# Hybrid decoder layer on one core: a sixth expert buffer elsewhere in SBUF, a new order in the last expert units, and two tiles of the last stage on VectorE alone

## The chip, the cores and the metric

The kernel runs on one core of a Trainium2 chip. The metric is the device time of one execution in microseconds. Engines: TensorE (PE in the profile; its weight loads are PEld), VectorE (DVE), ScalarE (ACT), GpSimd (POOL), SyncE (SP). SBUF and PSUM are the on-chip memories; a "bank" is one of eight PSUM banks of 128 x 512 f32.

## What is computed

One decoder layer over 1024 tokens of width 1024, all f32. Four mixers share the layer's input, then comes attention to a fixed memory, then a mixture of experts, then a final norm. The change touches the last two:

```python
h = _rmsnorm(x, norm_ffn[l])
x = x + hier_moe(h, w_rg[l], b_rg[l], w_re[l], b_re[l], w_e_gu[l], w_e_dn[l])
...
return _rmsnorm(x, norm_final)
```

`hier_moe` has each token choose one of 4 groups of 8 experts and two experts in it, each with a weight. An expert multiplies the row by `w_gu` (1024 x 512), takes `silu(gate) * up` (256 values), and multiplies by `w_dn` (256 x 1024). The two results, weighted, are added to x.

## The kernel before

**Up to the experts.** The first 750 us or so are the mixers, then come attention to the memory and the routing. The residual rows x2 (8 tiles of 128 tokens x 1024, 4 MB) are summed in the arena, one large SBUF tensor, at `o_bc`. For every tile SyncE stores the normed rows to DRAM (`xn_d`) and then x2 itself (`x2_d`, shown as `x_d` in the profile; `sp_tail`, L1197 and L1199), since the sixth weight buffer (`GU_AT[5]`, `DN_AT[5]`) lies over x2.

**The expert stage.** Tokens are sorted into 84 blocks of 32 slots. Four blocks make a unit, 21 units (`UN`) in all, numbered 0 to 20. Experts are ordered by load; the first have 3 or 4 blocks, the last 13 have 2 each. So the last units take two experts each: unit 18 the experts at places 26 and 27, unit 19 those at 28 and 29, unit 20 those at 30 and 31 (here simply "expert 28" and so on). Expert e uses buffer e mod 6. For one unit:

- GpSimd gathers 128 token rows from `xn_d` (L1836), TensorE transposes them (`tr`, L1569), VectorE scales them (`tokens`, L1347).
- `gate_up`: products with the gate-up weights into bank 2 or 6 (L1583), 2 MB of weights per expert.
- ScalarE takes silu (L1242), VectorE multiplies (L1356), TensorE transposes the result (`act_tr`, L1592), ScalarE copies it (L1246).
- `down`: products with the down weights, 1 MB per expert, into banks 4 and 5 (L1606).
- ScalarE and VectorE copy the result out (L1251, L1363), GpSimd scatters the rows to `y_d` in DRAM (L1847).

TensorE's order is written out in `pe_experts`: gate_up(u), act_tr(u-1), tr(u+1), down(u-1). ScalarE's and VectorE's orders (`act_experts`, `dve_experts`) have silu and gating of u ahead of the copies of u-1. SyncE loads weights (`sp_experts`, L1122 for gate-up, L1127 for down): when gate_up(u) is done, the gate-up weights for the buffers that become free; then, when down(u-1) is done, the down weights. At the end this gives the order of issue: gate-up 28 and 29, down 26 and 27, gate-up 30 and 31, down 28 and 29, down 30 and 31. All go through one hardware queue.

When down(18) is done SyncE issues `x2_back` (L1229), which brings x2 back into other places (`xb`). Then it reads a flag of slot overflow (not set here), loads the gain of the final norm (`fin_g`, L1989) and waits for all scatters (`pass_end`, L1150 and L1151).

**The last stage**, per tile m of 8: SyncE loads the two expert rows of each token (`yg[m]`, 1 MB, L1994; four at once, then one for each that lands). TensorE puts x2 into two banks by a product with the identity (`start`, L1960; the first four tiles before any y is there) and adds the first expert row times its weight by a product with a diagonal (`w_diag`, L1971). VectorE adds the second (L1941, two halves), ScalarE squares and takes the root (L1984, L1985), VectorE inverts (L2374) and scales by root and gain (L1952), SyncE stores (L1998, the last tile in halves, L2002). VectorE's order is: sum of m, then scaling of m-1.

## Time and profile before

| | |
|---|---|
| median of 3 runs | 1184.95 us (1183.56 to 1187.94) |
| the profiled execution's own time | 1186.36 us |
| its span in the trace | 1184.6 us |
| TensorE busy | 1116.2 us (94%) |
| VectorE busy | 538.4 us (45%) |
| ScalarE busy | 351.5 us (30%) |
| GpSimd busy | 117.3 us (10%) |
| DMA | 204.74 MB, mean 173 GB/s |
| share of the final chain | TensorE 73%, VectorE 10%, DMA 5% |

A busy share is a mean over stages that have different limits. The chain of waits, followed back from the last instruction, says which work ended last at each point; the windows give busy time, granted clock and DMA share of a stretch; the timeline gives single instructions, and in brackets how long the engine was idle before one and what ended that.

### The profile page before, as it was taken

How to read it: one execution, taken by the hardware profiler on the slowest of the kernel's cores; microseconds unless marked ns; L12 is line 12 of the kernel's file. 1: busy time of each engine (PE TensorE's matmuls, PEld its weight loads, DVE VectorE, ACT ScalarE, POOL GpSimd, SP SyncE). 2: the span in 40 equal slices, each digit the busy share in tenths (PEclk: the TensorE clock that was granted, in tenths of full speed). 3: DMA queues.
4: the chain of work that ended last, by engine and by line, in shares of the span. 5: the costliest groups of instructions: out<-in, count | busy, mean ns of one | idle time of the engine just before them, and what ended most of it. 6: DMA issues, size and time to landing. Idle time of an engine off the chain costs nothing.

```text
span 1184.6 us, 16485 instructions
## 1 busy us (share of the span) xinstructions
PE 1116.2 (94%) x6487; PEld 615.4 (52%) x6487; DVE 538.4 (45%) x1199; ACT 351.5 (30%) x676; POOL 117.3 (10%) x148
## 2 busy tenths in 40 slices
PE   6999999999999899988799999999999999999777
PEld 6545744444744589875465444456653333333223
DVE  6876333324399635596672222235442212121117
ACT  4114631111676423203664100165301111111004
POOL 2000012221000000001010000022111111111000
PEclk9999999999999899999989999999999999999889
DMA  8111022131113443330034000446388999999988
GB/s 285 37 57 56 14 82 69 64 97 50 36 36 134 190 129 84 132 144 1 3 141 178 0 1 1 148 173 236 117 290 342 413 390 421 421 424 421 423 322 353
DMA packets 67894, 204.74 MB, mean 173 GB/s; under 512 B 24573, under 2 KB 41185, under 8 KB 57313
## 3 DMA queue, kind: packets, MB, share of 16 engines
q1 hardware_dynamic: 61104, 186.64, 41.4%
q0 software_dynamic: 6656, 16.95, 3.8%
q8 instruction: 54, 0.88, 0.3%
q14 instruction: 32, 0.25, 0.1%
q10 hardware_dynamic: 48, 0.01, 0.0%
HBM read 171.58 MB, written 37.24 MB: 176 GB/s over the span
## 4 chain that ended last, share of the span: by engine, by line
PE 73%; DVE 10%; DMA 5%; issue 3%; ACT 3%; POOL 0%; SPq 0%; DVEq 0%; POOLq 0%; ACTq 0%
PE bank L2674 20%; PE bank L1583 11%; PE bank L1639 8%; PE bank L1606 5%; PE bank L1701 2%; PE bank L1654 2%; DMA arena<-in_w_e_gu 2%; DMA arena<-x_d 2%; PE bank L2801 2%; PE bank L805 1%; PE bank L916 1%; PE bank L1960 1%; PE bank L1569 1%; PE bank L866 1%; PE bank L853 1%
## 5 line engine op out<-in xcount | busy, mean ns | idle before, releaser
L2674 PE MATMUL bank<-arena 128*128 128x512 f32 (+3 forms) x1032 | 358.0, 506 | 8.1 <-ACT arena L2178 6.8
L2674 PEld LDWEIGHTS bank<-arena 128*128 128x128 f32 x1032 | 196.9, 192 | 163.0 <-issue 140.7
L1583 PE MATMUL bank<-arena 128*32 128x512 f32 x1344 | 150.4, 599 | 8.3 <-issue 7.3
L1583 PEld LDWEIGHTS bank<-arena 128*32 128x32 f32 x1344 | 44.8, 111 | 109.4 <-issue 109.4
L1639 PE MATMUL bank<-arena 128*128 128x512 f32 x220 | 95.6, 592 | 0.0
L2178 ACT ACTIVATE arena<-bank 128x512 f32<-128x512 f32 (+1 forms) x57 | 28.4, 504 | 167.3 <-PE bank L2674 166.8
L1606 PE MATMUL bank<-arena 128*32 128x512 f32 x672 | 76.5, 595 | 1.4 <-ACT arena L1246 1.4
L1356 DVE TENSOR_TENSOR arena<-arena,bank 128x256 f32<-128x256 f32 x21 | 8.9, 422 | 149.4 <-ACT arena L1242 149.4
L1399 DVE TENSOR_TENSOR arena<-arena,bank 128x512 f32<-128x512 f32 x32 | 22.0, 688 | 100.2 <-PE bank L1639 79.5
L1639 PEld LDWEIGHTS bank<-arena 128*128 128x128 f32 x220 | 41.3, 190 | 49.7 <-issue 49.7
L1242 ACT ACTIVATE arena<-bank 128x256 f32<-128x256 f32 x21 | 8.1, 383 | 156.7 <-PE bank L1583 156.7
L2164 ACT ACTIVATE arena<-arena 128x1024 f32<-128x1024 f32 x18 | 19.0, 1054 | 100.3 <-DVE arena L1399 95.0
L2445 DVE TENSOR_TENSOR arena<-arena,bank 128x512 f32<-128x512 f32 x35 | 23.3, 684 | 50.6 <-PE bank L2674 50.6
L1363 DVE COPY arena<-bank 128x512 f32<-128x512 f32 x21 | 14.5, 691 | 60.3 <-PE bank L1606 60.3
L1606 PEld LDWEIGHTS bank<-arena 128*32 128x32 f32 x672 | 20.0, 109 | 41.5 <-issue 39.2
L1251 ACT ACTIVATE arena<-bank 128x512 f32<-128x512 f32 x21 | 12.5, 597 | 85.8 <-PE bank L1606 85.8
L2615 DVE TENSOR_TENSOR arena<-arena,bank 128x512 f32<-128x512 f32 x24 | 16.5, 685 | 47.4 <-PE bank L2801 47.4
L805 PE MATMUL bank<-arena 64*128 64x128 f32 x448 | 32.7, 300 | 4.2 <-DVE arena L716 2.6
L716 DVE COPY_PREDICATED arena<-levT,bank 128x512 f32<-128x512 int32 x56 | 35.3, 710 | 0.7 <-PE bank L805 0.4
L1836 POOL DMA_INDIRECT arena<-xn_d,arena x21 | 21.4, 1017 | 138.1 <-PE bank L1569 121.5
L805 PEld LDWEIGHTS bank<-arena 64*128 64x128 f32 x448 | 29.6, 207 | 7.2 <-DVE arena L716 4.0
L1701 PE MATMUL bank<-arena 128*128 128x512 f32 x64 | 32.1, 625 | 0.9 <-DVE arena L1399 0.9
(408 smaller groups left out, 1564.2 us busy)
## 6 DMA issues: line engine op xcount, KB each, us to landing
arena<-in_w_e_gu SPq DMA_DIRECT2D x27, 2048.0 KB, 13.2
arena<-in_w_e_dn SPq DMA_DIRECT2D x32, 1024.0 KB, 13.5
arena<-in_w_in SPq DMA_DIRECT2D x11, 1024.0 KB, 5.2
arena<-y_d SPq DMA_DIRECT2D x8, 1024.0 KB, 11.1
arena<-hz_d SPq DMA_DIRECT2D x4, 1792.0 KB, 8.0
pk_d<-arena SPq DMA_DIRECT2D x8, 640.0 KB, 2.9
hz_d<-arena SPq DMA_DIRECT2D x4, 1280.0 KB, 4.9
arena<-in_w_e_gu SPq DMA_DIRECT2D x5, 1024.0 KB
```

What stands on the lines that cost most here:

```text
L716: v.copy_predicated(h_pm[it % 2][:, par], bc(levT[:, lv].bitcast(i32), 1, [P, 4, P]), scores).then_inc(s["h_pm"], 1)
L805: ins = mm(to, hz(it, lv)[rows(par), part], hz(it, lv)[rows(par), part], start=True, stop=True)
L1399: return v.tensor_tensor(part, part, bank[:, :], ALU.add)
L1583: ins = mm(bank[part, :], hgT[:, k, part], w_gu(buf(es[i]), k), start=(k == 0), stop=(k == KT - 1))
L1606: ins = mm(psum[4 + hf][part, :], actT[:, k, part], w_dn[buf(es[i])][:, k, cols], start=(k == 0), stop=(k == FE // P - 1))
L1639: ins = mm(psum[2 + u % 3][:, :], y_of(k, slice(m * P, (m + 1) * P)), wo[:, k, hf * HALF:(hf + 1) * HALF], start=(u >= 3 and k == W_ORDER[0]),
L1654: ins = mm(psum[Q_BANK[u]][:, :], mq[:, k, c * P:(c + 1) * P], hT[:, k, hf * HALF:(hf + 1) * HALF], start=(k == 0), stop=(k == KT - 1))
L1701: ins = mm(psum[3][:, :], m_oT[m % 2][:, c], mo[:, c, hf * HALF:(hf + 1) * HALF], start=(c == 0), stop=(c == CT - 1))
L2178: ins = nc.scalar.activation(dst, psum[PROJ_BANKS[u % 3]][0:rows, cols], ACT.Copy, scale=QK_SCALE if CHUNKS[UNITS[u][0]][1] == col["bq"] a ...
L2445: ins = v.tensor_tensor(to, to, bank, ALU.add)
L2674: ins = mm(psum[PROJ_BANKS[u % 3]][0:rows, 0:n], lhs(k), rhs(k), start=(k == 0), stop=(k == kt - 1))
L2801: ins = mm(psum[7][:, hp(h)], Qp[:, h], y[:, h], start=True, stop=True)
```

## The change

- Tables that are used only up to the routing (`triu`, `triu_s`, `tril_s`, `head_ones`, `levT`, `lru_w`, `memk`, `memv`) become slices of one tensor `early` of 3072 columns. The arena grows by 2048 columns; the space for that comes from halving the space for GpSimd's DMA descriptors (8192 bytes). The sixth buffer lies in `early`, in 1024 columns at the old end of the arena and in the new columns, so it no longer covers x2. `b_rank` and `toks_of` are placed in those 1024 columns.
- x2 is neither stored nor brought back. `y_out`, `yg`, `fin_g` and `w_diag` get other places; `fin_g` is loaded after gate_up(20).
- Before it loads buffer 5 the first time, SyncE waits for `t_r_dve` 6 instead of 4.
- At unit 20 TensorE does act_tr(19) and down(19) first and gate_up(20) then; ScalarE and VectorE likewise copy out unit 19 before silu and gating of unit 20.
- In the last stage tiles 4 and 7 (`SOLO`, the fifth and the last) are summed by VectorE alone, with two operations on 1024 columns in SBUF. TensorE works on the other six.

TensorE at the end of the expert stage, before (bank4, bank5: down; bank2: gate_up(20); bank3: act_tr; e_dn4 and x_cb are the semaphores of the down weights of experts 28 and 29, w_ld0 and w_ld1 those of the gate-up weights of experts 30 and 31):

```order
L1583 MATMUL bank2<-arena 32x512 [waits e_ac,e_ht,w_ld1,w_ld0]
L1583 MATMUL bank2<-arena 32x512 x15
L1583 MATMUL bank2<-arena 32x512 [waits e_ht]
L1583 MATMUL bank2<-arena 32x512 x15
L1592 MATMUL bank3<-ident,arena 128x128 [waits e_ats,e_ac]
L1592 MATMUL bank3<-ident,arena 128x128
L1606 MATMUL bank4<-arena 32x512 [waits e_ats,e_y,x_cb,e_dn4]
L1606 MATMUL bank4<-arena 32x512 x7
L1606 MATMUL bank5<-arena 32x512 x8
L1592 MATMUL bank3<-ident,arena 128x128 [waits e_ats,e_ac]
L1592 MATMUL bank3<-ident,arena 128x128
L1606 MATMUL bank4<-arena 32x512 [waits e_ats,e_y,e_dn1,e_dn0]
```

and with the change:

```order
L1584 MATMUL bank3<-ident,arena 128x128 [waits e_ats,e_ac]
L1584 MATMUL bank3<-ident,arena 128x128
L1598 MATMUL bank4<-arena 32x512 [waits e_ats,e_y,x_cb,e_dn4]
L1598 MATMUL bank4<-arena 32x512 x7
L1598 MATMUL bank5<-arena 32x512 x8
L1575 MATMUL bank2<-arena 32x512 [waits e_ac,e_ht,w_ld1,w_ld0]
L1575 MATMUL bank2<-arena 32x512 x15
L1575 MATMUL bank2<-arena 32x512 [waits e_ht]
L1575 MATMUL bank2<-arena 32x512 x15
L1584 MATMUL bank3<-ident,arena 128x128 [waits e_ats,e_ac]
L1584 MATMUL bank3<-ident,arena 128x128
L1598 MATMUL bank4<-arena 32x512 [waits e_ats,e_y,e_dn1,e_dn0]
```

The block of 32 products into bank2 moves behind the one that waits for e_dn4 and x_cb, and nothing stands any more between it and the last act_tr.

VectorE in the last stage at tile 4, before:

```order
L1941 SCALAR_TENSOR_TENSOR arena<-arena,bank7 128x512 [waits f_p]
L2374 RECIPROCAL rms<-rms 128x1 [waits rms_r]
L1952 SCALAR_TENSOR_TENSOR arena<-arena,rms,levT 128x1024 [waits v_chain]
L1941 SCALAR_TENSOR_TENSOR arena<-arena,bank0 128x512 [waits f_p,x_in0]
L1941 SCALAR_TENSOR_TENSOR arena<-arena,bank1 128x512 [waits f_p]
L2374 RECIPROCAL rms<-rms 128x1 [waits rms_r]
L1952 SCALAR_TENSOR_TENSOR arena<-arena,rms,levT 128x1024 [waits v_chain]
```

and with the change:

```order
L1943 SCALAR_TENSOR_TENSOR arena<-arena,bank7 128x512 [waits f_p]
L2376 RECIPROCAL rms<-rms 128x1 [waits rms_r]
L1954 SCALAR_TENSOR_TENSOR arena<-arena,rms 128x1024 [waits v_chain]
L1935 SCALAR_TENSOR_TENSOR arena<-arena 128x1024 [waits x_in0]
L1937 SCALAR_TENSOR_TENSOR arena<-arena 128x1024 [waits v_chain]
L2376 RECIPROCAL rms<-rms 128x1 [waits rms_r]
L1954 SCALAR_TENSOR_TENSOR arena<-arena,rms 128x1024 [waits v_chain]
```

The two halves that took TensorE's sums from bank 0 and bank 1 become two operations on whole rows in SBUF, the second linked to the first. The same happens at tile 7; all else keeps its order.

```diff
@@ -42,11 +42,10 @@
 
         ident = sb("ident", [P])
         ones = sb("ones", [P])
-        triu = sb("triu", [P])
-        triu_s = sb("triu_s", [P])
-        tril_s = sb("tril_s", [P])
-        head_ones = sb("head_ones", [P])
-        levT = sb("levT", [NL + 1, P])
+        early = sb("early", [3072])
+        triu, triu_s, tril_s, head_ones = [early[:, i * P:(i + 1) * P] for i in range(4)]
+        levT = early[:, 512:1536].rearrange("p (a b) -> p a b", a=NL + 1)
+        lru_w = early[:, 1536:2048].rearrange("p (a b) -> p a b", a=2 * CT)
         negmask = sb("negmask", [P])
         prow = sb("prow", [P])
...
@@ -1032,15 +1031,16 @@
         buf = lambda e: e % NB
         GU = KT * 2 * FE
         GU_AT = [((o_g2, 0, KT),), ((0, 0, KT),), ((EW, 0, KT),), ((o_g1, 0, KT),),
-                 ((o_g3, 0, 4), (o_tmp + 6 * D, 4, 6), (o_cx, 6, 8)), ((o_bc, 0, KT),)]
-        DN_AT = [o_g2 + GU, GU, EW + GU, o_g1 + GU, o_g1 + EW, o_bc + GU]
+                 ((o_g3, 0, 4), (o_tmp + 6 * D, 4, 6), (o_cx, 6, 8)), ((None, 0, 6), (48024 - 1024, 6, 8))]
+        DN_AT = [o_g2 + GU, GU, EW + GU, o_g1 + GU, o_g1 + EW, 48024]
+        piece = lambda off, n: early[:, 0:n] if off is None else arena[:, off:off + n]
         w_dn = [view(o, FE // P, D) for o in DN_AT]
 
         def w_gu(j, k):
 
             for off, k0, k1 in GU_AT[j]:
                 if k0 <= k < k1:
-                    return arena[:, off + (k - k0) * 2 * FE:off + (k - k0 + 1) * 2 * FE]
+                    return piece(off, (k1 - k0) * 2 * FE)[:, (k - k0) * 2 * FE:(k - k0 + 1) * 2 * FE]
 
         hg = [view(o_tmp + i * D, D) for i in range(2)]
@@ -1048,18 +1048,13 @@
         sg = view(o_tmp + 5 * D, FE)
         actv = view(o_tmp + 5 * D + FE, 2, FE)
         actT = view(o_tmp + 5 * D + 3 * FE, FE // P, P)
-        assert all(buf(e) not in (2, 3) for e in range(NE) if FIRST[e] + CAPS[e] > 4 * (UN - 2))
-        xb = [view(EW + m * D, D) for m in range(6)] + [view(o_g1 + m * D, D) for m in range(2)]
-        yg = [view(o + i * TK * D, TK, D) for o, n in ((0, 3), (o_g2, 3), (o_bc, 2)) for i in range(n)]
-        y_out = [view(o_g1 + (2 + i) * D, D) for i in range(6)] + [view(o_g3 + i * D, D) for i in range(2)]
-        fin_g = levT[:, :, :].rearrange("p a b -> p (a b)")
-        w_diag = view(o_tmp + 6 * D, NT, P)
+        yg = [view(i * TK * D, TK, D) for i in range(6)] + [view(o_g2 + i * TK * D, TK, D) for i in range(2)]
+        y_out = [view(o_g1 + i * D, D) for i in range(NT)]
+        fin_g = view(o_g3, D)
+        w_diag = view(o_g2 + 5 * D, NT, P)
 
         xn_d = nc.dram_tensor("xn_d", (T, D), f32, kind="Internal").ap()
         y_d = nc.dram_tensor("y_d", (TK * T, D), f32, kind="Internal").ap()
-        x2_d = nc.dram_tensor("x2_d", (NT, P, D), f32, kind="Internal").ap()
-        X2_STORED = 16 * (1 + NT)
-        X2_BACK = X2_STORED + 32
         moe = ({n: s["e_" + n] for n in
                                  "gu2 gu3 gu4 dn0 dn1 dn2 dn3 dn4 ix g0 g1 tr ht gu sg ac at ats dn y st0 st1".split()})
...
@@ -1195,24 +1190,17 @@
                     load_dn(sp, 3)
                 sp.wait_ge(s["xs_r"], G3 + m + 1)
                 sp.dma_start(xn_d[m * P:(m + 1) * P, :], xs[m % 2]).then_inc(s["t_xn"], 16)
-                sp.wait_ge(s["rms_r"], G3 + m + 1)
-                sp.dma_start(x2_d[m], x2[:, m]).then_inc(s["t_x2"], 16)
                 sp.wait_ge(s["t_xn"], 16 * (m + 1))
             sp.wait_ge(s["t_rl"], NT)
             sp.wait_ge(s["t_slt"], NT)
             load_gu(sp, 4, GU_AT[4][2:])
             load_dn(sp, 4)
-            sp.wait_ge(s["t_r_dve"], 4)
-            sp.wait_ge(s["t_x2"], X2_STORED)
+            sp.wait_ge(s["t_r_dve"], 6)
             sp.wait_ge(moe["g0"], 16)
             load_gu(sp, 5)
             load_dn(sp, 5)
             sp_experts(sp, moe, 0)
-            sp.wait_ge(moe["dn"], UN - 2)
-            x2_back(sp)
             with overflow(sp):
-                sp.wait_ge(s["t_x2"], X2_BACK)
-                pass_end(sp, moe, 0)
                 with sp.Fori(0, PASSES - 1) as p:
                     sp.wait_ge(moe["dn"], UN * (p + 1))
                     for e in range(NB):
...
@@ -1235,11 +1217,14 @@
             return eng.If(over > 0)
 
         def act_experts(act, q, p):
+            def gates(u):
+                act.wait_ge(q["gu"], UN * p + (u + 1))
+                after(act, q["ac"], UN * p, u)
+                nc.scalar.activation(sg, psum[2 + 4 * (u % 2)][:, 0:FE], ACT.Silu).then_inc(q["sg"], 1)
+
             for u in range(UN + 1):
-                if u < UN:
-                    act.wait_ge(q["gu"], UN * p + (u + 1))
-                    after(act, q["ac"], UN * p, u)
-                    nc.scalar.activation(sg, psum[2 + 4 * (u % 2)][:, 0:FE], ACT.Silu).then_inc(q["sg"], 1)
+                if u < UN - 1:
+                    gates(u)
                 if u >= 1:
                     b = (u - 1) % 2
                     act.wait_ge(q["at"], UN * p + u)
@@ -1249,6 +1234,8 @@
                     if u >= 3:
                         act.wait_ge((q["st0"], q["st1"])[b], gathered(u - 3, p))
                     nc.scalar.activation(ysb[b][:, 0:HALF], psum[4][:, :], ACT.Copy).then_inc(q["y"], 1)
+                if u == UN - 1:
+                    gates(u)
 
         def act_tail2(act, link, stats):
             for m in range(NT):
@@ -1348,12 +1335,15 @@
                                     bc(ffn_pk[:, 4 * k:4 * k + 4], 2, [P, 4, P]), ALU.mult).then_inc(q["ht"], 1)
 
             tokens(0)
+            def gated(u):
+                dve.wait_ge(q["sg"], UN * p + (u + 1))
+                after(dve, q["at"], UN * p, u - 1)
+                v.tensor_tensor(actv[:, u % 2], sg, psum[2 + 4 * (u % 2)][:, FE:2 * FE], ALU.mult).then_inc(q["ac"], 1)
+
             for u in range(UN + 1):
                 b = u % 2
-                if u < UN:
-                    dve.wait_ge(q["sg"], UN * p + (u + 1))
-                    after(dve, q["at"], UN * p, u - 1)
-                    v.tensor_tensor(actv[:, b], sg, psum[2 + 4 * b][:, FE:2 * FE], ALU.mult).then_inc(q["ac"], 1)
+                if u < UN - 1:
+                    gated(u)
                 if u + 1 < UN:
                     tokens(u + 1)
                 if u >= 1:
@@ -1361,6 +1351,8 @@
                     if u >= 3:
                         dve.wait_ge((q["st0"], q["st1"])[1 - b], gathered(u - 3, p))
                     v.tensor_copy(ysb[1 - b][:, HALF:D], psum[5][:, :]).then_inc(q["y"], 1)
+                if u == UN - 1:
+                    gated(u)
 
         def rows_from_table(v, step):
 
@@ -1609,13 +1601,16 @@
 
             tr(0)
             for u in range(UN + 1):
+                if u == UN - 1:
+                    act_tr(u - 1)
+                    down(u - 1)
                 if u < UN:
                     gate_up(u)
-                if u >= 1:
+                if u >= 1 and u != UN - 1:
                     act_tr(u - 1)
                 if u + 1 < UN:
                     tr(u + 1)
-                if u >= 1:
+                if u >= 1 and u != UN - 1:
                     down(u - 1)
 
         def rows_of_blocks(pe, mm):
...
@@ -1908,6 +1902,8 @@
             eng.wait_ge(sem, at + 16 * (m // 4 + 1))
 
         G4 = G3 + NT
+        SOLO = (4, 7)
@@ -1931,15 +1927,21 @@
             for m in range(NT):
                 ins = v.tensor_scalar(w_diag[:, m], ident[:, :], wts[:, 0, m:m + 1], None, ALU.mult)
                 ins.then_inc(s["t_r_dve"], 1) if m == NT - 1 else link(ins)
-            dve.wait_ge(s["x_row"], 17)
+            dve.wait_ge(s["t_x2"], 32)
             for m in range(NT + 1):
                 if m < NT:
                     y_wait(dve, m)
-                    for hf in range(2):
-                        dve.wait_ge(s["f_p"], 2 * m + hf + 1)
+                    if m in SOLO:
+                        link(v.scalar_tensor_tensor(x2[:, m], yg[m][:, 0], wts[:, 0, m:m + 1], x2[:, m], ALU.mult,
+                                                    ALU.add))
+                        v.scalar_tensor_tensor(x2[:, m], yg[m][:, 1], wts[:, 1, m:m + 1], x2[:, m], ALU.mult,
+                                               ALU.add).then_inc(s["f_c"], 2)
+                    for hf in range(2) if m in PAIRED else ():
+                        i = PAIRED.index(m)
+                        dve.wait_ge(s["f_p"], 2 * i + hf + 1)
                         cols = slice(hf * HALF, (hf + 1) * HALF)
-                        v.scalar_tensor_tensor(xb[m][:, cols], yg[m][:, 1, cols], wts[:, 1, m:m + 1],
-                                               psum[2 * (m % 4) + hf][:, :], ALU.mult, ALU.add).then_inc(s["f_c"], 1)
+                        v.scalar_tensor_tensor(x2[:, m, cols], yg[m][:, 1, cols], wts[:, 1, m:m + 1],
+                                               psum[2 * (i % 4) + hf][:, :], ALU.mult, ALU.add).then_inc(s["f_c"], 1)
                 if m >= 1:
                     q = m - 1
                     r = (G4 + q) % 4
@@ -1949,29 +1951,28 @@
                     else:
                         inverse_rms(G4 + q)
                         for cols in (slice(0, D),) if q < NT - 1 else (slice(0, HALF), slice(HALF, D)):
-                            v.scalar_tensor_tensor(y_out[q][:, cols], xb[q][:, cols], rms[:, r:r + 1], fin_g[:, cols],
+                            v.scalar_tensor_tensor(y_out[q][:, cols], x2[:, q, cols], rms[:, r:r + 1], fin_g[:, cols],
                                                    ALU.mult, ALU.mult).then_inc(s["xs_r"], 1)
 
         def pe_tail3(pe, mm):
-            def start(m):
+            def start(i):
                 for hf in range(2):
-                    if m >= 4:
-                        pe.wait_ge(s["f_c"], 2 * (m - 4) + hf + 1)
-                    mm(psum[2 * (m % 4) + hf][:, :], ident[:, :], xb[m][:, hf * HALF:(hf + 1) * HALF],
+                    if i >= 4:
+                        pe.wait_ge(s["f_c"], 2 * PAIRED[i - 4] + hf + 1)
+                    mm(psum[2 * (i % 4) + hf][:, :], ident[:, :], x2[:, PAIRED[i], hf * HALF:(hf + 1) * HALF],
                        start=True, stop=False)
 
             pe.wait_ge(moe["y"], 2 * UN)
-            pe.wait_ge(s["t_x2"], X2_BACK)
-            for m in range(4):
-                start(m)
+            for i in range(4):
+                start(i)
             pe.wait_ge(s["t_r_dve"], 7)
-            for m in range(NT):
+            for i, m in enumerate(PAIRED):
                 y_wait(pe, m)
                 for hf in range(2):
-                    mm(psum[2 * (m % 4) + hf][:, :], w_diag[:, m], yg[m][:, 0, hf * HALF:(hf + 1) * HALF],
+                    mm(psum[2 * (i % 4) + hf][:, :], w_diag[:, m], yg[m][:, 0, hf * HALF:(hf + 1) * HALF],
                        start=False, stop=True).then_inc(s["f_p"], 1)
-                if 4 <= m + 3 < NT:
-                    start(m + 3)
+                if 4 <= i + 3 < len(PAIRED):
+                    start(i + 3)
 
         def act_tail3(act, link, stats):
             for m in range(NT):
...
         def sp_tail3(sp):
-            sp.dma_start(fin_g, a["norm_final"].unsqueeze(0).to_broadcast([P, D])).then_inc(s["x_row"], 16)
+            sp.wait_ge(moe["gu"], UN)
+            sp.dma_start(fin_g, a["norm_final"].unsqueeze(0).to_broadcast([P, D])).then_inc(s["t_x2"], 16)
...
@@ -2856,7 +2858,7 @@
     import concourse.bacc as bacc
     from concourse.bass_utils import run_bass_kernel_spmd
 
-    nc = bacc.Bacc("TRN2", target_bir_lowering=False, num_devices=1)
+    nc = bacc.Bacc("TRN2", target_bir_lowering=False, num_devices=1, dynamic_dma_scratch_size=8192)
     arrays, aps = {}, {}
     for name in _INS:
         v = np.ascontiguousarray(inputs[name])
```

## Rows read from the trace of the kernel before

**Rows 1.** Windows: start:end, length, busy by engine, granted clock, DMA share, GB/s
```profile
850.00:900.00 50.00, 46.48 (x377) 27.11 (x380) 22.14 (x78) 7.01 (x14) 6.41 (x9) 1.00 0.75 272
900.00:950.00 50.00, 50.00 (x456) 17.72 (x452) 9.94 (x17) 5.79 (x13) 8.35 (x9) 1.00 0.99 391
...
1050.00:1100.00 50.00, 50.00 (x454) 18.43 (x450) 11.31 (x19) 6.23 (x14) 8.12 (x8) 1.00 1.02 424
```

**Rows 2.** Chain that ended last: start us, us, what
```profile
1102.96 5.02 issue
1107.98 9.19 PE bank L1583 x64
...
1122.86 23.63 DMA arena<-x_d
```

**Rows 3.** Weight loads by line, one or two issues each: duration ns, start us; landing
```profile
L1127 SPq DMA_DIRECT2D arena<-in_w_e_dn x1: 333/333/333, 1080.9 to 1080.9; - x1
...
DMA to landing us min/median/max: 33.2/33.2/33.2
...
L1122 SPq DMA_DIRECT2D arena<-in_w_e_gu x1: 2962/2962/2962, 1089.7 to 1089.7; - x1
...
DMA to landing us min/median/max: 34.1/34.1/34.1
...
L1127 SPq DMA_DIRECT2D arena<-in_w_e_dn x2: 1254/1804/2354, 1093.5 to 1096.6; - x2
```

**Rows 4.** Timeline of all engines, 1117 to 1142 us
```profile
1117.65 0.42 DVE L1356 TENSOR_TENSOR arena<-arena,bank 128x256 f32<-128x256 f32 x1 [14.36 <-ACT arena L1242]
...
1118.42 3.64 PE L1606 MATMUL bank<-arena 128*32 128x512 f32 x32
...
1123.96 7.08 PE L1583 MATMUL bank<-arena 128*32 128x512 f32 x64 [1.89 <-issue]
...
1132.14 3.64 PE L1606 MATMUL bank<-arena 128*32 128x512 f32 x32 [0.68 <-ACT arena L1246]
...
1135.72 0.50 PE L1592 MATMUL bank<-ident,arena 128*128 128x128 f32 x2
...
1136.97 3.64 PE L1606 MATMUL bank<-arena 128*32 128x512 f32 x32 [0.75 <-ACT arena L1246]
...
1141.63 0.97 POOL L1847 DMA_INDIRECT y_d<-arena  x1 [3.85 <-DVE arena L1363]
```

**Rows 5.** Windows of 5 us, columns as in rows 1
```profile
1105.00:1110.00 5.00, 2.02 (x12) 0.68 (x16) 0.00 (x0) 0.00 (x0) 0.00 (x0) 0.55 1.02 427
```

**Rows 6.** Chain that ended last, the first row gather
```profile
875.89 4.33 DMA arena<-xn_d,arena
```

**Rows 7.** Timeline of all engines, 1144 to 1183 us
```profile
1144.52 2.54 DVE L1932 TENSOR_SCALAR arena<-ident,arena 128x128 f32<-128x128 f32 x8 [3.16 <-issue]
...
1146.62 8.69 PE L1960 MATMUL bank<-arena,ident 128*128 128x512 f32 x16 [6.01 <-DMA arena<-x_d]
...
1148.29 12.68 SPq L1994 DMA_DIRECT2D arena<-y_d  x8
...
1156.33 1.49 DVE L1941 SCALAR_TENSOR_TENSOR arena<-arena,bank 128x512 f32<-128x512 f32 x2 [9.27 <-PE bank L1971]
...
1160.84 1.28 DVE L1952 SCALAR_TENSOR_TENSOR arena<-arena,rms,levT 128x1024 f32<-128x1024 f32 x1
...
1174.59 1.40 DVE L1941 SCALAR_TENSOR_TENSOR arena<-arena,bank 128x512 f32<-128x512 f32 x2
...
1177.30 1.40 DVE L1941 SCALAR_TENSOR_TENSOR arena<-arena,bank 128x512 f32<-128x512 f32 x2
...
1181.22 1.00 SPq L2002 DMA_DIRECT2D out<-arena  x2
```

**Rows 8.** DMA issues: the first y load and the last, us to landing
```profile
arena<-y_d SPq DMA_DIRECT2D x1, 1024.0 KB, 4.9
...
arena<-y_d SPq DMA_DIRECT2D x1, 1024.0 KB, 12.8
```

More of the change, by code:

```diff
@@ L1015, in hybrid_trunk @@
         over_i = kp(1).bitcast(i32)
[L1017 to L1018 removed]
+        rw = region(48024 - 1024, 48024)
+        rx = region(o_tmp + 7168, 48024 - 1024)
+        b_rank, b_hit = rw(NRO, NBL), rx(NRO, NBL)
         b_rank_i = b_hit.bitcast(i32)
[L1020 removed]
+        toks_of = [rw(BT * TK, NE) for _b in range(2)]
         slotT = rx(P)
@@ L1910, in hybrid_trunk @@
         G4 = G3 + NT
+        SOLO = (4, 7)
+        PAIRED = [m for m in range(NT) if m not in SOLO]
         POOLED = ()
```

22 lines of the change are left out of this document (6 added, 16 removed).

## The prediction

> **What bounds the kernel now.** I read the windows first. From 900 us to the end of the expert stage TensorE is busy all the time and the DMA engines are as well, at 391 to 424 GB/s; between 850 and 900 us the DMA share is only 0.75 [rows 1]. So the stage has two bounds side by side, and traffic that is over before 900 us has left no queue behind it. Next, the chain that ended last: it shows where the balance tips. TensorE stands still before gate_up(19), which then runs 9.19 us, and later the chain sits 23.63 us on the return of the residual rows (x_d) [rows 2]. The timeline of the last two units [rows 4] and the landings of the last weights [rows 3] say which weight each wait is for, and the timeline of the last stage [rows 7] gives the pace of VectorE there.
>
> One reading matters before anything is costed. The x_d return ends the wait of TensorE at 1146.62, but the eight y loads are issued only at 1148.29, when the last scatter has landed [rows 7]. x_d stands in the chain, yet taking it away alone would bring the y loads no earlier.
>
> **Part 1: the residual rows stay on the chip.** Gone are eight stores of 512 KB and two loads of 4 MB together. The stores came before the first gather, where the DMA share was 0.75 [rows 1]: worth nothing, since the stage behind them starts with the first gather and with buffers, not with a queue. The loads were issued behind every weight, at about 1122.5, landing 23.63 us later [rows 2]; they delayed no weight. What they did cost: TensorE's first eight starting products of the last stage waited 6.01 us and took 8.69 us [rows 7], and the last scatter shared the engines with them. That scatter took from 1141.63 [rows 4] to 1148.29 [rows 7], 6.66 us. A 512 KB gather at a quiet moment took 4.33 us [rows 6]. After the change the last scatter meets only fin_g. The two ends are 4.33 and 6.66 us; I take 5.3, between them because a scatter writes DRAM and the gather did not: **-1.35 us**, ends -2.3 and 0.
>
> The page "DMA: Bandwidth & Descriptors" of the Trainium skill (section on the anatomy of one DMA) fits a software-generated transfer as 2.0 us plus bytes over 436 GB/s, about 3.2 us for 512 KB as an estimate. The gather's row is 1.1 us over it, so the trace does not agree; by the page alone this term would be -3.5 us.
>
> The sixth buffer moves to other addresses and its load becomes two pieces, five more issues on SyncE, each under 3 us [rows 3] and each made while some 33 us of loads are queued [rows 3]: nothing. SyncE now waits for t_r_dve 6 in place of 4; the gather wait behind it is later (the first gather lands at 880.2 [rows 6]): nothing. GpSimd's descriptor space is halved; each of its indirect transfers holds it 0.97 us [rows 4], and I cost it at nothing, since no row of it waits for an earlier transfer. fin_g is loaded after gate_up(20), some 10 us before it is read.
>
> **Part 2: unit 19 finished before gate_up(20).** Here the order on TensorE meets the order of the loads. Before, TensorE left down(18) at 1122.06 (1118.42 + 3.64), waited 1.89 us for the gate-up weights of expert 31, and ran gate_up(20); down(19) followed at 1132.14, released by ScalarE and not by a DMA [rows 4]. Those weights of expert 31 were issued at 1089.7 and landed 34.1 us later, at 1123.8; the down weights of experts 28 and 29, which down(19) needs, were issued behind them, at 1093.5 and 1096.6 [rows 3]. Now down(19) is asked for first, at 1122.06 + 1.25 = 1123.3 (1.25 us from transposing actv to the product: 1135.72 to 1136.97 [rows 4]). Is expert 29 there? No row shows its landing. Two estimates: from the down weights of expert 27 (1080.9 + 33.2 = 1114.1) to expert 31 at 1123.8, 4 MB took 9.7 us [rows 3], so 2 MB more take 4.8 us: 1128.7. And with the age of its neighbours, 33.2 to 34.1 us, 1096.6 gives about 1130.2. I take 1129.5; the ends are 1123.3 (there in time) and 1132.14, when down(19) ran without waiting for it.
>
> So TensorE stands from about 1122.6 to 1129.5 with gate_up(20)'s weights already in place. Everything of unit 20 is queued behind: products, gate, scatter, the y loads. A stop of 5.4 us brought the granted clock to a mean of 0.55 in 1105 to 1110 [rows 5], that is to its lower level, 1.2 GHz, for part of it; gate_up(19) took 9.19 us against 7.08 [rows 2, 4], 2.1 us more. I charge that once more; its ends are 0 and 2.1.
>
> The sum from 1129.5: down(19) 3.64, gate_up(20) 7.08, slow clock 2.1, then gating, which now stands in the open. Before, down(19) covered it. From the end of gate_up(19), 1117.17, to the end of VectorE's gating, 1118.07, is 0.90 us [rows 2, 4], plus 1.25 to the product: 2.15. Then down(20) 3.64 and 1.02 to the scatter (1140.61 to 1141.63 [rows 4]). 1129.5 + 19.6 = 1149.1 against 1141.63: **+7.5 us**.
>
> **Part 3: VectorE alone on tiles 4 and 7.** Let Y be the issue of the first y load, before 1148.29. Before, the first sum ran at Y + 8.04, because the starting products had ended only at 1155.31, and the end came at Y + 36.3. Now those products need only the last evacuation, so the first y tile decides: Y + 4.9 [rows 8], plus 1.02 from TensorE's product to the sum: Y + 5.9. From there, VectorE's own steps: 4.51 to the first scaling (1156.33 to 1160.84), 1.2 to the third sum, then 2.71 per tile (1174.59 to 1177.30) [rows 7]. A tile summed from SBUF costs two operations of the 1.28 us kind [rows 7] instead of 1.40 for the two halves: +1.16. Hence the last sum starts at 5.9 + 4.5 + 1.2 + 5 x 2.71 + 1.16 = 26.3. The last y tile lands at Y + 25.2 (issued last in SyncE's 12.68 us, about 1160.7 [rows 7], landing 12.8 us later [rows 8]), so it is in time. From the last sum to the end took 7.3 us, now 8.5 with the second 1.16: Y + 34.8, **-1.5 us**. TensorE loses two tiles of work, but it is not what the last tiles waited for; the two extra 1.16 take back most of what the earlier start gives. Ends: -2.5 (the third sum too gets ahead) and +0.6 (the first sum stays at Y + 8).
>
> **The sum.** -1.35 + 7.5 - 1.5 = +4.7 us on the profiled span of 1184.6 (its execution took 1186.36, the median of the runs is 1184.95). On the median: **1189.7 us**. About 0.5%, 5.9 us, is what a measurement of this kernel can tell from no change, so the forecast is "no change", on the slow side.
>
> **The rivals.**
> (a) *Slower: VectorE binds the last stage.* If the starting products still delay the first sum beyond Y + 7.4 (36.3 - 28.9, the new path from first sum to end), part 3 turns into a cost. TensorE has a check of the overflow flag before them; VectorE's first operation behind its own came 3.16 us late [rows 7], and the clock is low there too. With +0.6 for the tail and no gain on the scatter: +7.5 + 0.6 = +8.1, **1193.1 us**. For it: VectorE's two 1.16 are certain. Against: y needs 4.9 us to land.
> (b) *Faster: the down weights are there.* Then unit 19's products run from 1123.3 with no slow clock, the scatter goes out at 1123.3 + 17.5 = 1140.8, and -0.8 - 1.35 - 1.5 gives -3.7, **1181.3 us**. For it: no row shows the landing. Against: issued 7 us after a load that landed at 1123.8. The same page of the skill (section on queues, rings and completion order) has each engine consume a queue's descriptors in ring order, though one may finish its write ahead of another; by it (b) would hardly occur, and the rows 3 agree as far as they reach: 1114.1, then 1123.8, in order of issue.
> (c) *A queue that I cost at nothing matters*: if the stores do leave a queue, the weights come earlier by their 4 MB, at 424 GB/s [rows 1] 9.9 us: no stop before gate_up(19) (-5.0 and -2.1 [rows 2]), none before down(19) as in (b), so 1181.3 - 7.1 = 1174.2 us. Against: the DMA share of 0.75 behind the stores [rows 1].
>
> **Chances.** Forecast 0.52, (a) 0.23, (b) 0.17, (c) and the unnamed 0.08. The forecast's own terms reach from 1184.8 (weights at 1128.7, full clock, best ends of parts 1 and 3) to 1195.7; a quarter of it lies above 1190.9, as does nearly all of (a): slower 0.35. Faster than 1179.0 needs (c) or the best ends of (b): 0.10. Within: 0.55. The range takes in (b) and (a): 1180.5 to 1194.
>
> **What would show it.** Right: before down(19) in the new profile a wait of TensorE of 5 to 8 us that ends with a load of in_w_e_dn, a granted clock of about 0.5 behind it, gate_up(20) starting near 1133, no x_d, y loads issued near 1154, VectorE with no gaps from the third tile on and the end some 35 us after the first y load. Wrong: down(19) starting before 1126 breaks part 2; a first sum later than 7.4 us after the y loads means (a); any shift of the first gather at 876 means that I mis-costed the stores.

## The result, and the profile after

| | before | changed |
|---|---|---|
| median | 1186.74 us (1183.56 to 1189.81, 17 executions) | 1189.91 us (1185.88 to 1195.13, 17 executions) |
| ratio, 95% interval | | 1.0031 [1.0020, 1.0042] |
| the profiled execution / its span | 1186.36 / 1184.6 us | 1189.96 / 1188.2 us |
| DMA | 204.74 MB | 196.35 MB |

The medians differ by 3.2 us, and the ratio says 0.3% with an interval that leaves out zero, below the 0.5% that the text above calls measurable. "No change, on the slow side" was the forecast, at 1189.7 us. The forecast stood on the median of three runs, 1184.95 us; over the 17 executions the kernel before has 1186.74.

The profile after starts with a shift that has to be taken out first. The timeline of GpSimd at the first gather, in the changed kernel:

```profile
873.90 1.18 POOL L1830 DMA_INDIRECT arena<-xn_d,arena  x1 [16.34 <-DVE arena L1360]
```

Before, it stood at 875.89. Below I therefore count from the first gather, and call that G; whether the 2.0 us belong to the change is a question for the controls.

Timeline of TensorE at the end of the expert stage, changed kernel (start us, us, engine, line, operation, count, and in brackets the idle time before and what ended it); it answers to [rows 4]:

```profile
1105.95 1.07 PE L1575 MATMUL bank<-arena 128*32 128x512 f32 x2 [5.42 <-issue]
...
1115.99 3.64 PE L1598 MATMUL bank<-arena 128*32 128x512 f32 x32
...
1127.60 6.48 PE L1598 MATMUL bank<-arena 128*32 128x512 f32 x32 [7.53 <-DMA arena<-in_w_e_dn]
1133.89 7.06 PE L1575 MATMUL bank<-arena 128*32 128x512 f32 x64
1141.91 0.51 PE L1584 MATMUL bank<-ident,arena 128*128 128x128 f32 x2 [0.96 <-DVE arena L1341]
1143.10 3.64 PE L1598 MATMUL bank<-arena 128*32 128x512 f32 x32 [0.68 <-ACT arena L1231]
1148.59 7.15 PE L1962 MATMUL bank<-arena,ident 128*128 128x512 f32 x16 [1.85 <-issue]
```

Up to down(18) nothing has changed: gate_up(19) is at G+232.05 (before G+232.09, the same stop ahead of it), down(18) at G+242.09 (G+242.53). Then comes the new stop, 7.53 us, ended by the down weights, and down(19) takes 6.48 us for the 32 products that take 3.64 elsewhere. gate_up(20) starts at G+259.99; before, it was at G+248.07. The last rows show gating in the open: from the end of gate_up(20) to down(20) TensorE does 0.51 us of work.

Windows of the same stretch, columns as in [rows 1]:

```profile
1120.00:1125.00 5.00, 0.07 (x1) 0.00 (x0) 0.39 (x1) 0.57 (x2) 0.97 (x1) 0.81 0.92 386
1125.00:1130.00 5.00, 2.40 (x12) 0.69 (x16) 0.00 (x0) 0.00 (x0) 0.00 (x0) 0.50 0.56 230
1130.00:1135.00 5.00, 5.00 (x36) 1.45 (x32) 0.69 (x1) 0.60 (x1) 0.00 (x0) 0.66 0.07 29
1135.00:1140.00 5.00, 5.00 (x52) 1.50 (x48) 0.00 (x0) 0.00 (x0) 0.97 (x1) 1.00 0.18 70
```

TensorE is empty for 5 us, the clock falls to 0.50 (1.2 GHz), and from 1130 on the DMA engines have nothing left to bring (29 GB/s). All weights are there, and the products that could have run meanwhile are only starting.

The chain of waits of the changed kernel, which answers to [rows 2]:

```profile
1093.81 33.69 DMA arena<-in_w_e_dn
1127.60 6.52 PE bank L1598 x32
1136.08 11.45 issue
1147.76 4.21 DMA y_d<-arena
1152.37 6.87 DMA arena<-y_d
```

The return of x2 (x_d) is out of it. In its place stands the load of the down weights, issued at 1093.81 and landed at 1127.5, then the last scatter, then the y loads. The last stage, from the timelines of SyncE, GpSimd and VectorE [rows 7]:

```profile
1147.76 0.98 POOL L1841 DMA_INDIRECT y_d<-arena  x1 [11.69 <-DVE arena L1353]
1151.99 12.57 SPq L1996 DMA_DIRECT2D arena<-y_d  x8
...
1158.12 1.49 DVE L1943 SCALAR_TENSOR_TENSOR arena<-arena,bank 128x512 f32<-128x512 f32 x2 [4.84 <-PE bank L1972]
...
1162.64 1.28 DVE L1954 SCALAR_TENSOR_TENSOR arena<-arena,rms 128x1024 f32<-128x1024 f32 x1
1163.96 1.54 DVE L1943 SCALAR_TENSOR_TENSOR arena<-arena,bank 128x512 f32<-128x512 f32 x2
...
1167.39 1.54 DVE L1943 SCALAR_TENSOR_TENSOR arena<-arena,bank 128x512 f32<-128x512 f32 x2 [0.51 <-PE bank L1972]
...
1170.24 1.28 DVE L1935 SCALAR_TENSOR_TENSOR arena<-arena 128x1024 f32<-128x1024 f32 x1
1171.63 1.29 DVE L1937 SCALAR_TENSOR_TENSOR arena<-arena 128x1024 f32<-128x1024 f32 x1
...
1174.22 1.40 DVE L1943 SCALAR_TENSOR_TENSOR arena<-arena,bank 128x512 f32<-128x512 f32 x2
...
1179.64 1.28 DVE L1935 SCALAR_TENSOR_TENSOR arena<-arena 128x1024 f32<-128x1024 f32 x1
```

The scatter lands 4.23 us after its issue (6.66 before), the first sum comes 6.13 us after the y loads (8.04), but the end comes 36.2 us after them, as before (36.3). Between the tiles VectorE still waits for TensorE (0.51 at 1167.39), so of the 1.9 us that the first sum is ahead, the last sum, 27.65 us after the y loads and not 29.01, keeps 1.4. The last solo tile gives most of this back: its two operations take 2.67 us (1179.64 to 1182.31) where two halves take 1.40.

So the ledger of the two profiles is: last scatter G+273.86 against G+265.74, **+8.1**; its landing **-2.4**; last stage **-0.1**; together +5.6, less 2.0 for the early shift, gives the +3.6 us of the spans.

### The profile page after: what moved, and what is told of

It reads as the page before. It is cut to its first block, busy times and chain, and to the rows that moved or that the text cites. A ratio compares the mean times of both kernels' runs of the same rounds, so it can differ in the third digit from the quotient of the medians.

```text
span 1188.2 us, 16457 instructions
## 1 busy us (share of the span) xinstructions
PE 1109.1 (93%) x6471; PEld 609.9 (51%) x6471; DVE 540.5 (45%) x1199; ACT 351.7 (30%) x676; POOL 117.4 (10%) x148
## 2 busy tenths in 40 slices
DMA packets 66405, 196.35 MB, mean 165 GB/s; under 512 B 24492, under 2 KB 41104, under 8 KB 55824
## 4 chain that ended last, share of the span: by engine, by line
PE 71%; DVE 11%; DMA 4%; issue 4%; ACT 3%; SPq 1%; POOL 0%; DVEq 0%; POOLq 0%; ACTq 0%
PE bank L2676 20%; PE bank L1575 10%; PE bank L1634 8%; PE bank L1598 5%; DMA arena<-in_w_e_dn 3%; PE bank L1696 2%; PE bank L1649 2%; PE bank L2803 2%; PE bank L803 1%; PE bank L914 1%; PE bank L1561 1%; PE bank L864 1%; PE bank L1716 1%; PE bank L851 1%; PE bank L882 1%
## 5 line engine op out<-in xcount | busy, mean ns | idle before, releaser
L1634 PE MATMUL bank<-arena 128*128 128x512 f32 x220 | 95.6, 592 | 0.0
L1575 PE MATMUL bank<-early,arena 128*32 128x512 f32 x168 | 39.0, 615 | 0.0
L714 DVE COPY_PREDICATED arena<-early,bank 128x512 f32<-128x512 int32 x56 | 35.4, 719 | 0.6 <-PE bank L806 0.3
```

The lines of the kernel that those rows point to most:

```text
L714: v.copy_predicated(h_pm[it % 2][:, par], bc(levT[:, lv].bitcast(i32), 1, [P, 4, P]), scores).then_inc(s["h_pm"], 1)
L1575: ins = mm(bank[part, :], hgT[:, k, part], w_gu(buf(es[i]), k), start=(k == 0), stop=(k == KT - 1))
L1634: ins = mm(psum[2 + u % 3][:, :], y_of(k, slice(m * P, (m + 1) * P)), wo[:, k, hf * HALF:(hf + 1) * HALF], start=(u >= 3 and k == W_ORDER[0]),
```

## The experiments

Every kernel was run beside the kernel before on the same chip; a ratio is to that, and for each there are 6 to 12 executions. All compute the full result; four of them add filler products (the 128x128 identity against itself, repeated to 512 columns) into a PSUM bank that nobody reads.

### Parts alone

Two kernels with the old unit order (the three `u == UN - 1` special cases taken out), one of them also without solo tiles, and the changed kernel without solo tiles:

```diff
-        SOLO = (4, 7)
+        SOLO = ()
```

**x2 kept on the chip, alone** (old order, no solo tile):

> The change without its new order (gate_up(20) ahead of down(19) again) and without VectorE alone on tiles 4 and 7: what is left is that x2 stays on the chip and the sixth buffer lies elsewhere. Theory (the wait for expert 29's down weights is the cost, the rest gains): last scatter as in before (7 us after the first product of down(20) less than 5 us), y loads 4.2 us after it instead of 6.7, and first sum 6.1 us after the y loads, so some 3.6 us faster than before, ratio 0.997; 6 to 7 us faster than the changed kernel. Rival 1 (the new addresses and the load in two pieces cost): no faster than before, the wait ahead of gate_up(19) or gate_up(20) longer than 5.4 and 1.9 us. Rival 2 (the early tables in one tensor bring 2 us before the first gather, as the profile of the changed kernel has it at 873.9 against 875.9): first gather near 873.9 again, and 5 to 6 us faster than before.

Measured: 1181.26 us, 0.9952 [0.9935, 0.9969]. That is 5.6 us under the kernel before and not 3.6, and the first gather is at 873.88: both are the numbers of rival 2, to which the controls come back. The last scatter is at G+268.05, behind a gate_up(20) of 8.77 us.

**Old order, solo tiles kept:**

> The changed kernel with the old order in the last units alone; tiles 4 and 7 stay with VectorE. Theory: TensorE no longer waits 7.5 us for in_w_e_dn and down(19) takes 3.64 us instead of 6.5; the last scatter goes out 8 us earlier and the kernel is 6 to 8 us faster than the changed one, 1.5 to 3 us faster than before (ratio 0.998). Rival (the two solo tiles are the cost, 36.2 us from the y loads to the end): the time stays within 2 us of the changed kernel's.

Measured: 1182.01 us, 0.9958 [0.9942, 0.9974]: 7.9 us under the changed kernel's median. Taking the new order back turns the change from a loss into a gain, of 4.8 us and not the 1.5 to 3 that I expected.

**New order, no solo tile:**

> The changed kernel with no tile left to VectorE alone (TensorE works on all eight), the new order kept. Theory: TensorE's pace of 3.43 us a tile binds up to tile 5, VectorE behind it; the last sum starts 27.7 us after the first y load as in the changed kernel, but takes 1.40 instead of 2.6, so 1.2 us faster than the changed kernel (ratio to before 1.002). Rival (the solo tiles bring what they were meant to): 2 to 3 us slower than the changed kernel.

Measured: 1190.26 us, 1.0027 [1.0014, 1.0039]. Its last stage ends 35.5 us after the y loads, 0.7 us better than with the solo tiles (36.2); the first kernel here shows the same against the second (35.6 and 36.2). Without them three sums in a row, from the fourth tile to the sixth, wait 0.5 us each for TensorE, and the last sum starts 28.05 us after the y loads: the solo tiles bring it 0.4 us forward, and the last of them takes 1.3 us more. The executions show no difference: the solo tiles cost 0.7 us in the profiles and nothing that the times can tell. This kernel and the first one, run beside each other, differ in the order alone: 1190.26 against 1181.26 us, so that with x2 on the chip the new order costs 9.0 us by these medians, or 6 with the repeat of the first kernel below (ratios 1.0027 and 0.9976).

**The new order alone**, in the kernel before:

```diff
+                if u == UN - 1:
+                    act_tr(u - 1)
+                    down(u - 1)
                 if u < UN:
                     gate_up(u)
-                if u >= 1:
+                if u >= 1 and u != UN - 1:
                     act_tr(u - 1)
```

> The kernel before with the new unit order alone; x2 is still stored and brought back, all eight tiles on the old path. Theory (the order costs what the down weights of expert 29 make it wait): TensorE waits 6 to 8 us before down(19) on a load of in_w_e_dn, the last scatter is issued 273.5 to 274.5 us after the first gather (before: 265.7), and 8 us are lost there. Given back: the return of x2, issued when down(18) is done, has landed by then, so the scatter lands after 4.2 to 4.6 us and not 6.7, and the first y sum comes 6 us after the y loads and not 8. Against the kernel before about +4.5 us, ratio 1.004, as the whole change. Rival (the order costs nothing by itself, the moved buffer or the split load does): no wait over 2 us before down(19), ratio 1.000 or less.

Measured: 1188.80 us, 1.0022 [1.0013, 1.0032]. TensorE's timeline:

```profile
1127.89 5.46 PE L1616 MATMUL bank<-arena 128*32 128x512 f32 x32 [6.77 <-DMA arena<-in_w_e_dn]
1133.16 7.06 PE L1593 MATMUL bank<-arena 128*32 128x512 f32 x64
```

The stop comes with the order, without any moved buffer. The last scatter is at G+272.4, 1.1 us earlier than expected, and lands after 4.39 us though x2 is still brought back: by then that load is over. So the new order, late as it is, already takes the price of the return of x2 off the path, and keeping x2 on the chip can't gain it a second time. The time, +2.6 us by the ratio, is under the +4.5 that I expected.

### Is it the place in the queue, or the open chain?

SyncE issues the down weights of experts 28 and 29 ahead of the gate-up weights of experts 30 and 31:

```diff
             for u in range(UN):
+                if u != UN - 4:
+                    gate_ups(u)
...
+                if u == UN - 4:
+                    gate_ups(u)
```

> The changed kernel, but SyncE issues the down weights of experts 28 and 29 ahead of the gate-up weights of experts 30 and 31. Theory (loads land in order of issue and at the pace of the queue, so down(19) waits only for its place in it): down(19) runs right behind act_tr(19) without a wait of more than 1 us, gate_up(20) now waits for expert 31 by 1 to 3 us, last scatter 266 to 268.5 us after the first gather (changed kernel: 273.9), 6 to 7 us faster than the changed kernel, ratio to the kernel before about 0.998. Rival (unit 19's chain in the open is dear by itself): the last scatter stays later than 271 and the ratio at 1.001 or more.

Measured: 1183.63 us, 0.9990 [0.9981, 1.0000]. The timelines of SyncE and TensorE:

```profile
1089.98 1.37 SPq L1122 DMA_DIRECT2D arena<-in_w_e_dn  x1
1092.17 4.74 SPq L1117 DMA_DIRECT2D arena<-in_w_e_gu  x2
...
1120.31 3.64 PE L1604 MATMUL bank<-arena 128*32 128x512 f32 x32 [0.76 <-ACT arena L1237]
1126.71 7.08 PE L1581 MATMUL bank<-arena 128*32 128x512 f32 x64 [2.75 <-issue]
```

The down weights of expert 29 are issued at 1089.98 and land 26.3 us later, at 1116.3, which is G+242.9; in the changed kernel, where they are issued at 1093.81, it is G+253.6. 3.8 us in the issue are 10.7 us in the landing. The gate-up weights of expert 31 pay for it: they land at G+253.3 in place of G+247.9. down(19) follows its own act_tr, released by ScalarE and not by a load; gate_up(20) now waits, 2.75 us, and the last scatter is at G+267.25. Both numbers lie inside what was expected. 6.6 of the 8.1 us, the slow down(19) among them, hung on nothing but which weights were issued first. What is left is 1.5 us: gate_up(20) starts at G+253.36, 5.3 us later than before, since its weights now come behind those of unit 19, and down(19), which is no longer behind it, gives 3.8 of that back. In the changed kernel the order in which weights are asked for and the order in which they are used had gone apart.

### The slow clock behind the stop

Filler products between act_tr(19) and down(19), in the changed kernel, first 15, then 8:

```diff
                 if u == UN - 1:
                     act_tr(u - 1)
+                    for _i in range(15):
+                        mm(psum[7][:, :].rearrange("p (a b) -> p a b", b=P), ident[:, :],
+                           bc(ident[:, :], 1, [P, 4, P]), start=True, stop=True)
                     down(u - 1)
```

> The changed kernel with 15 products of 128x128 by 128x512 into the unused bank 7 between act_tr(19) and down(19), some 6.45 us of work that nobody reads. Theory: they fill the wait for the down weights, the granted clock stays at 1.00 in the 5 us before and after down(19), and down(19) takes 3.64 us instead of 6.5: 2.8 us faster than the changed kernel; the wait's end does not move. Rival (down(19)'s 6.5 us are its weights still landing in SBUF, or products slowed by DMA, and not the clock): down(19) stays at 6 us or more. If the weights land before the fill is through, the gain is smaller by that.

Measured with 15: 1194.30 us, 1.0076 [1.0053, 1.0099], slower than the changed kernel, against what I expected. The timeline gives a part of the reason:

```profile
1118.66 13.04 PE L1607 MATMUL bank<-ident 128*128 128x512 f32 x30
1131.63 3.64 PE L1598 MATMUL bank<-arena 128*32 128x512 f32 x32
```

I had taken half the length for a filler: each is two products, 0.87 us. They end at G+258.3, 4.6 us after the weights landed in the changed kernel (G+253.7). down(19) does take 3.64 us, so 2.8 us come back, and the scatter is 1.8 us later: 4.6 - 2.8. The medians are 4.4 us apart, and what makes the rest no trace shows.

> The changed kernel with 8 filler products between act_tr(19) and down(19). In the run with 15 they lasted 13.0 us, 0.87 us each, past the landing of the weights; 8 last 6.9 us and end within the stop of 7.5 us. Theory (the slow clock behind the stop costs 2.8 us): down(19) starts with the landing of its weights as in the changed kernel, 253.7 us after the first gather, and takes 3.6 and not 6.5 us; 2.8 us faster than the changed kernel, ratio to the kernel before 1.0005 to 1.001. Rival (the fall comes from something else, or VectorE and ScalarE set the pace of unit 19): down(19) still takes over 5 us, or the scatter comes no earlier; ratio 1.003.

Measured with 8: 1187.38 us, 1.0018 [1.0002, 1.0035]:

```profile
1122.94 7.03 PE L1607 MATMUL bank<-ident 128*128 128x512 f32 x16
1129.90 3.64 PE L1598 MATMUL bank<-arena 128*32 128x512 f32 x32
```

down(19) takes 3.64 us and starts 0.9 us later, right behind the fillers (G+254.6; they began late, since gate_up(19) had been slower in this execution); the scatter is at G+271.9, 1.9 us earlier: 2.8 - 0.9. The granted clock is 1.00 in every window from 1115 to 1135, where the changed kernel has 0.50 between 1125 and 1130. The times agree in sign, but the intervals of this kernel and of the changed one overlap. The traces show the clock's share: 2.8 of the 8.1 us. It is a part of the 6.6 above and does not come on top.

With the old order the same is tried ahead of the products that wait there, 5 fillers before gate_up(19) and 4 before gate_up(20):

> Old unit order, no tile summed by VectorE alone, x2 kept on the chip, and fillers while TensorE waits for weights: 5 (4.35 us) before gate_up(19), 4 (3.5 us) before gate_up(20). Theory (the slow clock of gate_up(20), 8.77 against 7.08 us, is on the path; that of gate_up(19) is not, since gate_up(20) then waits for its weights anyway): gate_up(19) and gate_up(20) take 7.1 us each, the last scatter 266.4 us after the first gather (without fillers 268.1), 1.7 us faster than the same kernel without them, ratio to the kernel before about 0.994. Rival: the fillers delay the products behind them by more than the clock gives back; ratio 0.996 or more.

Measured: 1182.37 us, 0.9973 [0.9964, 0.9982]. In its profile both gate_ups take 7.1 us and the last scatter is at G+265.67, as expected; the times do not show the 1.7 us that I expected. Two fillers before gate_up(20) alone:

> The same with 2 filler products (1.74 us) ahead of gate_up(20), where TensorE waits 2.5 us; none before gate_up(19). Theory (a slow gate_up(20) costs 1.7 us in the executions that have it): gate_up(20) 7.1 us in the profile, last scatter about 266.4 us after the first gather, up to 1.7 us faster than the kernel without fillers, ratio 0.994 to 0.9955. Rival (fillers cost as much as they bring, as the run with 9 of them had it by its times): ratio 0.9965 or more.

Measured: 1180.38 us, 0.9967 [0.9951, 0.9982]; last scatter at G+265.62. The ratio is that of the rival. The profiles of the old order without fillers (the two above and the two below) may explain it: gate_up(20) takes 8.77 us in two of them and 7.08 in the other two, so that there is not always a slow clock to mend.

### Controls

The kernel with x2 kept alone once more, the same with the eight stores of x2 put back, and the kernel before against itself:

> The same without the stores, a second time (first time 0.9952, interval 0.9935 to 0.9969). Theory: 0.9945 to 0.997, gate_up(20) at 7.1 or 8.8 us by the draw of the clock, last scatter 266 to 268.5 us after the first gather, end 35.3 to 35.8 us after the y loads. Rival (the first result was a lucky set of executions): 0.9975, as 3.1 us of gain from the scatter's landing and the tail alone would give.

Measured: 1182.12 us, 0.9976 [0.9965, 0.9987]. That is the rival's number: the first result, 0.9952, was the better of two by 2 us or more. The two sets of executions ran on two chips, and no run tells the draw of the executions from the chip. The two profiles of this one kernel differ in two places. Timeline of TensorE, first profile:

```profile
403.71 21.31 PE L2669 MATMUL bank<-arena 128*128 128x260 f32 x96 [1.36 <-ACT arena L2173]
...
1122.56 8.77 PE L1571 MATMUL bank<-arena 128*32 128x512 f32 x64 [2.48 <-issue]
```

and second profile:

```profile
403.03 24.24 PE L2669 MATMUL bank<-arena 128*128 128x260 f32 x96 [2.94 <-ACT arena L2173]
...
1123.61 7.08 PE L1571 MATMUL bank<-arena 128*32 128x512 f32 x64 [1.79 <-issue]
```

The early group, which the change does not touch, takes 21.31 or 24.24 us, and G comes at 873.88 or 875.79. The first profiles of before and of the changed kernel differ in the same way: that group takes 24.24 us before and 21.31 after, and from a group of 16 products near 765 us to G both need 109.0 us (766.88 to 875.89, 764.86 to 873.90). So the early 2.0 us of the changed kernel's profile are a draw of the execution and not a part of the change, and rival 2 of the first kernel falls.

> x2 kept on the chip with the old unit order and all tiles on the old path, but with the eight stores of x2 to DRAM put back (nothing reads them). Theory (the stores were worth nothing, their time is hidden): the same time as the kernel without them, ratio to the kernel before 0.995 to 0.9975, within 0.15% of the next kernel; 60 us ahead of the first gather nothing moves. Rival (a queue from the stores or their waits was worth 2 us or more): ratio 0.998 or above, clearly over the next kernel's, and a later first gather relative to the last starting work of the routing.

Measured: 1181.83 us, 0.9970 [0.9959, 0.9981], within 0.1% of the kernel without the stores. From the start of that same group of 16 products to G both have 109.0 us (764.76 to 873.76, and 766.78 to 875.79). The stores were hidden.

> The kernel before itself, once more, as a control. Ratio 1.000 within 0.001. Theory (the times of before hold executions in which gate_up(20) ran at the low clock; the profile shown of before drew a fast one): this profile shows gate_up(20) at 8.8 us or the first gather near 874.5 us and not 875.9. Rival (7.1 us is the rule in the kernel before, 8.8 us in the ones without the return of x2): gate_up(20) 7.1 us again.

Measured: 1185.69 us, 1.0008 [0.9995, 1.0021]. Last scatter at G+265.54, gate_up(20) 7.08 us, the end 36.0 us after the y loads, and G at 874.90: from G on the second profile of before repeats the first, and G moves here too. My guess about gate_up(20) was wrong; that G would come earlier was right.

## Why the prediction was right, point by point

| step | predicted | changed kernel's profile |
|---|---|---|
| last scatter lands after | 5.3 us | 4.23 us |
| down(19) starts, on the clock of before | 1129.5 | 1129.6 (G+253.70) |
| slow clock there | 2.1 us | 2.8 us |
| last scatter issued | +7.5 us | +8.1 us |
| first sum after the y loads | 5.9 us | 6.13 us |
| last sum after the y loads | 26.3 us | 27.65 us |
| end after the y loads | 34.8 us | 36.2 us |
| sum | +4.7 us | +5.6 us; by the times +3.7 (ratio) or +3.2 (medians) |

**Part 1** was right in what it named and too small: the scatter's landing fell to 4.23 us, the pace of the quiet gather (4.35 us in this profile), so that here a scatter into DRAM was about as dear as a gather out of it. The reason for which I had stayed at 5.3 us, that a scatter writes DRAM, did not hold. The page "DMA: Bandwidth & Descriptors" of the Trainium skill (the anatomy of one DMA) would give about 3.2 us for it, as an estimate; the scatters that meet no load, 3.99 to 4.86 us, stay over that. That the stores cost nothing was shown by the kernel that puts them back, and that the new place of the buffer and the halved descriptor space cost nothing by the repeat of the kernel with x2 kept alone, whose last scatter is at G+265.50 (before: 265.74). Alone, Part 1 gives -3.0 us by its second profile's terms (landing 4.55 for 6.66 us, last stage 35.66 for 36.31, scatter 0.2 earlier) and -2.8 by its times.

**Part 2** is where the change loses, and it went as told: the wait, its releaser, the landing to 0.1 us, the low clock, the open gating. The error is the clock's term. A product of this kind takes 3.64 / 32 = 0.11 us at the full clock and, at half of it, 0.23 as an estimate, so the 2.1 us that I took over from gate_up(19) are some 18 slow products, and the 2.84 us of down(19) some 25 of its 32. The other two profiles with this stop and no filler have 6.10 us behind 7.94 of waiting and 5.46 behind 6.77, so the size of this term varies from profile to profile. The order experiment shows this part alone, and the swapped loads show that its cause is the place of the down weights in the queue. Rival (b) fell, as its row on the order of issue said. The page "DMA: Bandwidth & Descriptors" of the Trainium skill (queues, rings and completion order) says that on each DMA engine the descriptors of a queue are consumed in ring order, though a later one may finish its write first. The trace agrees as far as landings can show it: gate-up 30 and 31, then down 28 and 29 land at 1116.9, 1121.8, 1124.3 and 1127.5, as they were issued, and with the issues swapped the down weights land first.

**Part 3** had one step wrong: "then 2.71 per tile" from the third sum on. From the third to the fourth sum 3.43 us pass (1163.96 to 1167.39), because VectorE waits for TensorE there: +0.7. Around the first solo tile another 0.25 us are lost, 0.1 of it because its two operations take 2.68 us (1170.24 to 1172.92) and not twice 1.28, and the third sum itself is 0.4 late; these make the 1.35 us at the last sum. The step from TensorE's pace to VectorE's was in my own rows of before, at the tiles that I had not quoted. Rival (a) was no better: the first sum came at 6.13 and not beyond 7.4 us. But part 3 came out at -0.1 us, nearer to the +0.6 of (a) than to the -1.5 of the forecast.

**The sum.** Part 1 brought 1.05 us more than forecast, part 2 cost 0.6 more and part 3 brought 1.4 less: +5.6 us by terms, in which the errors cancel in part, and +3.7 [2.4 to 5.0] by the ratio of the times. That the median, 1189.91 us, lies within 0.2 us of the forecast of 1189.7 is luck: on the 1186.74 us that before has over the 17 executions the same sum would have said 1191.4. The early draw of 2.0 us explains the +3.6 us of the profiles but not the medians. The other kernels with the new order come out better by their ratios than by such terms too: order alone +3.8 (6.6 - 2.3 - 0.5) against +2.6, no solo tile +4.7 against +3.2, 8 fillers +4.6 against +2.1; the one with 15 fillers does not (+8.0 against +9.0). I have no trace that shows why, and leave it open; a part may be the scatter between sets, since before against itself gave 1.0008.

## What to carry to other kernels

When work is moved forward on an engine, move what it waits for forward in the transfer queue as well: at the end of this expert stage, where loads landed 25 to 34 us after their issue, they landed in the order in which they were issued, and the engine idled on one transfer while the data of the work that it used to do lay ready. An item that stands in the chain of waits (here the return of x2, 23.63 us) is worth only what separates it from the next one to end; the kernels with the old order show that at 3 to 6 us. Compare profiles from a point behind which the change can act, since what lies before differed by up to 3.5 us from profile to profile.

## What the runs showed of the hardware that I had not expected

- The first gather came between 872.84 and 876.39 us in the profiles of this study, and at 873.88 and 875.79 in two profiles of one kernel. One group of 96 products near 400 us, the same in all kernels, took 21.31 us in twelve profiles and 24.24 in two. From the group near 765 us to the first gather it is 109.0 us in eleven profiles and 110.5 to 110.7 in three (no solo tile, 8 fillers, old order with solo tiles), whose edits do not reach that stretch. These differences are as large as what was to be measured.
- A wait does not settle the clock behind it by its length alone. In the old order gate_up(20) took 7.08 us after waits of 1.79 to 1.96 us and 8.77 us after 2.41 and 2.48 us, but 7.08 us after 2.75 us in the kernel with swapped loads, where another 3.64 us of products had run at full clock shortly before.
- Fillers hold the clock for the products behind them in all four traces (gate_up at 7.1 us, down(19) at 3.64) and bring little in the times: in the old order 0.9973 and 0.9967 with them, 0.9976 and 0.9952 without.
- No version beats the others for certain: x2 on the chip with the old unit order, with or without solo tiles or fillers, lies between 1180.4 and 1182.4 us, 3 to 6 us under the kernel before beside it and 7.5 to 9.5 under the changed one.
